# Experts' weight slots given back by their own last product, the spreading in two parts, and chunk-wise rows in the layers

## The chip, the core and the metric

The kernel runs on one core of one Trainium2 chip. The metric is the device time of one execution in microseconds (us), as the median of three runs. TensorE (PE) multiplies, VectorE (DVE) and ScalarE (ACT) move and transform what it leaves in the eight PSUM banks, GpSimd (POOL) does small steps of the norms, and SyncE (SP) issues the DMA transfers that bring the weights from HBM.

## The reference, cut to what matters

The input is x of 256 rows by 1024, and all numbers are fp32. First comes one block: a mixer, a cross attention to 256 rows of memory and a mixture of 32 experts, each added to x. Then come two layers, each with a mixer of three branches (a Hyena convolution, a gated linear attention, pooling) and a feed-forward part of width 2816, with norms before and after. The part on which most of this text turns is the mixture of experts, two of the 32 for each row:

```python
    expert_id = g_idx * EXPERTS_PER_GROUP + e_local
...
    def expert_block(args):
        xb, e = args
        return (jax.nn.silu(xb @ w_gate[e]) * (xb @ w_up[e])) @ w_down[e]
...
    contrib = (w_sorted[:, None] * y_disp[dest].astype(jnp.float32))
    out = jnp.zeros((T, D), jnp.float32).at[t_sorted].add(contrib)
```

An expert's w_gate and w_up are 1024x512 and its w_down is 512x1024, so that each expert has 6 MB of weights and all of them 192 MB.

## The kernel before

**The stages.** The first block up to its experts fills the first 272 us of the span, the experts follow until about 720 us, the first layer until 1203 us, the second until 1669 us, and a short end of norms and the store of the output closes it. Each engine has its program written out by hand. Between engines stand semaphores; the eight PSUM banks are handed out in turn by a recorder (`opened`, `close`, `taken_up`, `done`), whose waits the views of the order show as `filled` (TensorE is done with a bank) and `taken` (the bank has been read).

**The experts.** There are eight passes of four experts. Each expert takes at most 32 of its rows in a pass, so that the four of a pass lie side by side in four column groups of TensorE. The weights of a pass come in 12 slots of 2 MB: four for gate (c = 0 to 3), four for up, four for down (f = 0 to 3); each holds a quarter of that matrix for all four experts. The SP queue fills seven or more places in turn, and issues into a place once `w_used` of it is counted (L4403). On TensorE `expert_pass` does eight products a slot (`mm` with a 128x32 left side and 512 columns; kk = 0, 1 and the expert q = 0 to 3). A released slot is only put into a list (`release`), and the next product that passes through `first_mm` carries its signal.

**The fifth block of rows.** One expert of each pass, the fullest, gets a further block of 32 rows. VectorE copies this expert's part of each slot (128x1024, `more_slot`, L2814, semaphore `more_copied`), since which expert it is is known at run time only. `more_products` on TensorE (right side "const" or "zone") uses two such copies at a time and signals `more_used`, after which VectorE may copy the next two. TensorE waits for the copy of each slot before it gives the slot back:

```python
                    more_slot(4 * i + c)
                    release(at)
```

**Around the gate slots of passes 1 to 7** stand other steps: `in0` and `in1` gather the rows of the pass (VectorE scales `in1` in `rows_in`, L2876); `more_in` gathers those of the fifth block (32 products with 32 columns, evacuated on L2890); `spread` brings the results of the pass before back to their places in x, for row tile t = 0 and t = 1 (`own_rows`, `more_rows`), and `add_rows` on VectorE (L2972) adds them; `weights_T` transposes the weights of the rows, `weights_out` copies them (L2884) and then picks and weighs the rows of the next pass (`place`, L2736 and L2743); `more_weights` does so for the fifth block (L2782). Pass 7 has no such spreading in it, since pass 6 spreads its own at its end.

**The layers.** `quad` in `pe_layer` (L3168) is one step of a matrix product on halves: sums and row sums are made by VectorE (`sums`, `tsum`), partial products are held in SBUF by ScalarE (`held`, L3579). The norm ahead of the feed-forward part ("m") ends on VectorE with one scaling of 128x1024 for each row tile (L4183), TensorE transposes the tile into two banks (`norm_tile_T`), ScalarE copies these with the gain (four 128x128, L2003), and the products `ff20` and `ff21` of row tile 0 begin after both. The transposes of row tile 1 follow behind them. In the quad `QK_QUAD` ScalarE also does two Exp (L3608) and two Ln (L3611, `low_rank`) of 128x1024 between its held copies.

The functions that the diff touches:

## Time and profile before

| what | value |
|---|---|
| median of three runs (lowest, highest) | 1692.74 us (1691.36, 1692.76) |
| the profiled execution: its time, its span | 1691.05 us, 1688.9 us |
| TensorE busy | 1635.9 us, 97% of the span |
| VectorE busy, ScalarE busy | 60%, 19% |
| read from HBM | 395.22 MB |

The span is what the profile covers; the execution's time is 2.15 us longer. A busy TensorE is not one at its peak: the ends of its instructions are modelled, and products in different column groups overlap.

### The profile page before, as it was taken

How to read it: one execution, taken by the hardware profiler on the slowest of the kernel's cores; microseconds unless marked ns; L12 is line 12 of the kernel's file. 1: busy time of each engine (PE TensorE's matmuls, PEld its weight loads, DVE VectorE, ACT ScalarE, POOL GpSimd, SP SyncE). 2: the span in 40 equal slices, each digit the busy share in tenths (PEclk: the TensorE clock that was granted, in tenths of full speed). 3: DMA queues.
4: the chain of work that ended last, by engine and by line, in shares of the span. 5: the costliest groups of instructions: out<-in, count | busy, mean ns of one | idle time of the engine just before them, and what ended most of it. 6: DMA issues, size and time to landing. Idle time of an engine off the chain costs nothing. (4 is left out here: it accounts for less than half of the span.)

```text
span 1688.9 us, 26924 instructions
## 1 busy us (share of the span) xinstructions
PE 1635.9 (97%) x11364; PEld 1218.6 (72%) x11364; DVE 1010.8 (60%) x1654; ACT 324.9 (19%) x758; POOL 25.3 (1%) x49
## 2 busy tenths in 40 slices
PE   9999999999988999999999999999999999999998
PEld 8777975443433344398799969994798999699953
DVE  4767445344433433369656677766688566677675
ACT  2332222100000000113232122110233221121100
POOL 0010000000000000000000000000000000000000
PEclk9999999997998999999999999999999999999999
DMA  9323388999999999945322524533534143433540
GB/s 364 153 102 149 150 374 328 400 429 427 427 428 427 427 427 426 425 176 199 150 100 107 203 116 200 200 154 133 212 138 180 71 198 144 183 153 147 200 174 25
DMA packets 30635, 398.03 MB, mean 236 GB/s; under 512 B 3505, under 2 KB 4145, under 8 KB 5810
## 3 DMA queue, kind: packets, MB, share of 16 engines
q1 hardware_dynamic: 29938, 393.66, 57.1%
q10 hardware_dynamic: 576, 2.62, 0.4%
q8 instruction: 92, 1.51, 0.4%
q14 instruction: 29, 0.24, 0.0%
HBM read 395.22 MB, written 1.05 MB: 235 GB/s over the span
## 5 line engine op out<-in xcount | busy, mean ns | idle before, releaser
L1249 PE MATMUL bank<-zone,w 128*128 128x128 f32 (+1 forms) x5632 | 659.9, 279 | 4.7 <-ACT zone L2003 1.7
L1249 PEld LDWEIGHTS bank<-zone,w 128*128 128x128 f32 x5632 | 649.6, 192 | 15.2 <-issue 5.9
L1249 PE MATMUL bank<-zone 128*128 128x128 f32 (+7 forms) x3220 | 478.0, 415 | 11.4 <-DMA zone<-in_w_experts 4.0
L1249 PE MATMUL bank<-w,zone 128*32 128x512 f32 (+2 forms) x1736 | 425.1, 581 | 10.1 <-DMA w<-in_w_experts 8.3
L1249 PEld LDWEIGHTS bank<-zone 128*128 128x128 f32 (+2 forms) x3220 | 308.6, 169 | 169.0 <-issue 139.6
L1249 PEld LDWEIGHTS bank<-w,zone 128*128 128x128 f32 (+1 forms) x1736 | 197.6, 156 | 207.2 <-issue 183.7
L2012 ACT ACTIVATE zone<-bank 128x512 f32<-128x512 f32 (+2 forms) x97 | 52.7, 561 | 420.7 <-PE bank L1249 314.6
L3833 DVE TENSOR_TENSOR w<-w 128x1024 f32<-128x1024 f32 x88 | 103.5, 1218 | 0.0
L3579 ACT ACTIVATE zone<-bank 128x256 f32<-128x256 f32 x88 | 33.7, 385 | 216.9 <-PE bank L1249 216.9
L3841 DVE TENSOR_TENSOR zone<-bank,zone 128x256 f32<-128x256 f32 x88 | 36.3, 422 | 61.7 <-PE bank L1249 34.5
L2814 DVE TENSOR_SCALAR zone<-w 128x1024 f32 x52 | 34.8, 689 | 61.4 <-PE bank L1249 45.4
L3833 DVE TENSOR_TENSOR w<-zone,w 128x1024 f32<-128x1024 f32 x44 | 52.9, 1222 | 20.4 <-PE bank L1249 20.4
L1299 PEld LDWEIGHTS bank<-const,zone 128*128 128x128 f32 (+2 forms) x256 | 28.0, 146 | 41.1 <-DVE zone L2814 11.8
L3833 DVE TENSOR_TENSOR zone<-w 128x1024 f32<-128x1024 f32 x44 | 52.0, 1218 | 3.2 <-DMA w<-in_w_layers 3.1
L2814 DVE TENSOR_SCALAR zone<-zone 128x1024 f32 x42 | 28.2, 688 | 41.1 <-PE bank L1249 31.7
L1299 PE MATMUL bank<-const,zone 128*128 128x128 f32 (+2 forms) x256 | 37.5, 281 | 14.2 <-DVE zone L2814 5.7
L1249 PE MATMUL bank<-zone,const 128*32 128x512 f32 (+2 forms) x284 | 44.9, 643 | 4.3 <-DVE const L2890 4.3
L2972 DVE TENSOR_TENSOR x<-bank,x 128x512 f32<-128x512 f32 x32 | 20.6, 686 | 43.4 <-PE bank L1249 43.4
L3841 DVE TENSOR_TENSOR zone<-bank,held 128x256 f32<-128x256 f32 x44 | 18.5, 424 | 43.2 <-PE bank L1249 42.8
L3786 DVE TENSOR_SCALAR zone<-zone,vec 128x256 f32<-128x256 f32 x68 | 27.9, 410 | 14.1 <-ACT zone L3765 10.9
L4354 POOL TENSOR_TENSOR stat<-stat 128x1 f32<-128x1 f32 (+2 forms) x28 | 17.1, 612 | 1162.2 <-DVE stat L3025 456.4
L3788 DVE SCALAR_TENSOR_TENSOR zone<-zone,vec 128x256 f32<-128x256 f32 x68 | 33.0, 485 | 2.4
(321 smaller groups left out, 978.5 us busy)
## 6 DMA issues: line engine op xcount, KB each, us to landing
w<-in_w_layers SPq DMA_DIRECT2D x66, 2048.0 KB, 8.8
w<-in_w_experts SPq DMA_DIRECT2D x52, 2048.0 KB, 21.5
zone<-in_w_experts SPq DMA_DIRECT2D x42, 2048.0 KB, 23.4
w<-in_w_first SPq DMA_DIRECT2D x15, 2048.0 KB, 8.8
w<-in_w_layers SPq DMA_DIRECT2D x4, 1536.0 KB, 6.3
w<-in_w_layers SPq DMA_DIRECT2D x4, 1024.0 KB, 6.5
w<-in_w_first SPq DMA_DIRECT2D x2, 1024.0 KB, 7.1
zone<-in_w_split SPq DMA_DIRECT2D x2, 1024.0 KB, 8.7
```

The source lines that it names most:

```text
L1249: return eng.matmul(out, lhsT, rhs, start=start, stop=stop, **kw_)
L1299: ins = eng.transpose(bank[0:m, at:at + n], src, idn)
L2012: A(dst, src, func, **k).then_inc(*banks.done(pl, name))
L2814: V.tensor_scalar(more_part(pl.region, n), spots[at].rearrange("p (q n) -> p q n", q=EPI)[:, bass.ds(q, 1), :].rearrange("p a n -> p (a n) ...
L2972: V.tensor_tensor(xs, banks.tile(pl, f"{pre}{t}{n}"), xs, ALU.add).then_inc(*banks.done(pl, f"{pre}{t}{n}"))
L3579: A(carried[name][:, g], banks.tile(pl, f"sx{p}{g}")[:, 0:T].rearrange("p (i t) -> p i t", i=2), ACT.Copy).then_inc(*pl.up(sem("held")))
L3786: v(pl, V.tensor_scalar(dst, src[:, 0:T], pv(layer, wname, 3 * c), pv(layer, bname, c), ALU.mult, ALU.add))
L3788: V.scalar_tensor_tensor(dst, src[:, 2:T + 2], pv(layer, wname, 3 * c + 2), dst, ALU.mult, ALU.add).then_inc(*pl.up(signal))
L3833: V.tensor_tensor(to, l, r, op).then_inc(*pl.up(sem("sums")))
L3841: return V.tensor_tensor(quad_rows(p, g, second, t), bank, carried[name][:, g], ALU.add)
L4354: eng.tensor_tensor(rstd[:, at:at + n], ms[:, col:col + n], mhalf[:, 0:n], ALU.pow).then_inc(*pl.up(sem("rstd")))
```

## The change

**In the experts, on TensorE.** The wait for the copy of a slot stands before the slot's last product (q = 3 of kk = 1, in down q = 3 of the second half) and no longer behind it, and this last product itself signals `w_used`. The last slot of gate, of up and of down, whose last product closes a bank, still gives its slot back by the next product; with gate and up the wait moves there too, while with the last slot of down it stays behind.

**In the gate slots of passes 1 to 7.** Before, `spread` of both row tiles, `weights_T`, `more_in` and the first `more_products` stood between c = 1 and c = 2. Now only `more_in` stands there; the first `more_products` are within c = 2; `spread` of row tile 0 stands behind c = 2; the second `more_products`, `spread` of row tile 1 and `weights_T` stand behind c = 3. VectorE's steps follow this order. The results of the fifth block lie in another place until they are spread (`more_ye`).

**In the layers.** The quads wait for each row sum by itself. In norm "m" VectorE scales in halves, ScalarE signals each 128x128 of row tile 0 (`first_rows`), TensorE goes through `ff20` and `ff21` together, k by k, and the transposes of row tile 1 stand behind the first product group of the first up quad. The second Ln stands behind one held copy.

```diff
@@ -1774,31 +1776,41 @@
                         for evacuated in banks.taken_up(gp, f"in{c // 2}"):
                             eng.wait_ge(*evacuated)
                     for kk in range(2):
-                        if pass0 and (kind, c, kk) == ("gate", 3, 1):
+                        if (kind, c, kk) == ("gate", 3 if pass0 else 2, 1):
                             more_products(kind, part, 1)
                         for q in range(EPI):
                             r = q * CAP
+                            if (kk, q) == (1, EPI - 1):
+                                more_slot(4 * i + c)
                             ins = mm(bank[r:r + CAP, :], Xg[:, 2 * c + kk, r:r + CAP],
                                      w[:, q * 1024 + kk * FE:q * 1024 + (kk + 1) * FE], c == 0 and kk == 0, c == 3 and kk == 1)
-                            if (c, kk, q) < (3, 1, EPI - 1):
+                            if (kk, q) < (1, EPI - 1):
                                 first_mm(pl, ins)
                     if c == 3:
                         ins.then_inc(*banks.close(pl, kind))
-                    more_slot(4 * i + c)
-                    release(at)
+                    else:
+                        ins.then_inc(*pl.up(sem(f"w_used{at}")))
+                    if c == 3:
+                        release(at)
                     if pass0 and (kind, c) == ("up", 0):
                         weights_T(1)
-                    if not pass0 and (kind, c) == ("gate", 1):
+                    if not pass0 and kind == "gate" and c >= 2:
+                        if c == 3:
+                            more_products(kind, part, 3)
                         if spreading:
-                            spreading.pop()(pl, "prev")
-                        weights_T(0)
+                            spreading[0](pl, "prev", [c - 2])
+                        if c == 3:
+                            weights_T(0)
+                            if spreading:
+                                banks.skip(pl, 3)
+                            spreading.clear()
                     if (kind, c) == ("gate", 2 if pass0 else 1):
                         eng.wait_ge(*pl.need(sem("more_picked"), 1))
                         group(pl, "more_in", [((P, k * CAP, CAP), [(hs[:, t, k * P:(k + 1) * P], Pm_in[:, t, :]) for t in range(TT)])
                                               for k in range(KT)])
                     if c == (2 if pass0 and kind == "gate" else 1):
                         part = opened(pl, f"more_{kind}")
-                    if c % 2 == 1 and not (pass0 and (kind, c) == ("gate", 1)):
+                    if c % 2 == 1 and not (kind == "gate" and (c == 1 or not pass0)):
...
@@ -1807,14 +1819,18 @@
             bank = [opened(pl, f"down{n}") for n in range(2)]
             for evacuated in banks.taken_up(pl, "hid"):
                 eng.wait_ge(*evacuated)
-            def down_half(f, half, cols):
+            def down_half(f, half, cols, freeing=None):
                 for q in range(EPI):
                     r = q * CAP
+                    if f < 3 and (half, q) == (1, EPI - 1):
+                        more_slot(8 + f)
                     ins = mm(bank[half][r:r + CAP, :], hidT[:, f, r:r + CAP], cols(q), f == 0, f == 3)
-                    if f < 3 or q < EPI - 1:
+                    if q < EPI - 1 or (f, half) < (3, 0) and half == 0:
                         first_mm(pl, ins)
                 if f == 3:
                     ins.then_inc(*banks.close(pl, f"down{half}"))
+                elif half == 1:
+                    ins.then_inc(*pl.up(sem(f"w_used{freeing}")))
...
-            def spread(to, pre):
+            def spread(to, pre, tiles=range(TT)):
                 for evacuated in banks.taken_up(pl, "weights", "down0", "down1"):
                     eng.wait_ge(*evacuated)
-                for t in range(TT):
+                for t in tiles:
...
-                    down_half(f, half, lambda q: (kept, w)[half][:, q * 512:(q + 1) * 512] if split else w[:, q * 1024 + half * 512:q * 1024 + (half + 1) * 512])
-                more_slot(8 + f)
-                release(at)
+                    down_half(f, half, lambda q: (kept, w)[half][:, q * 512:(q + 1) * 512] if split else w[:, q * 1024 + half * 512:q * 1024 + (half + 1) * 512], at)
+                if f == 3:
+                    more_slot(8 + f)
+                    release(at)
...
@@ -2001,6 +2018,8 @@
                 if gname:
                     for c in range(4):
                         ins = A(dst[:, c, t * P:(t + 1) * P], bank[:, c, :], ACT.Copy, scale=pv(layer, gname, c))
+                        if (pre, t) == ("m", 0) and c < 3:
+                            ins.then_inc(*pl.up(sem("first_rows")))
...
@@ -2924,12 +2943,14 @@
                 rows_in(pl)
                 more_slot(pl, q, 0)
                 more_slot(pl, q, 1)
-                if i < PASSES - 1:
-                    add_rows(pl, banks, pre="prev")
+                more_in()
+                for t in range(TT):
+                    more_slot(pl, q, 2 + t)
+                    if i < PASSES - 1:
+                        add_rows(pl, banks, [t], "prev")
                 weights_out()
-                more_in()
                 more_weights(pl, e)
-                for n in range(2, 8):
+                for n in range(4, 8):
...
-                eng.wait_ge(*pl.need(sem("tsum"), 8 if p in UP_QUADS else 4))
+                eng.wait_ge(*pl.need(sem("tsum"), row_sum + 1))
...
@@ -3433,14 +3458,27 @@
         release(two[0])
         out_product(out_sums["S1"], tsum[:, 0], "l5")
         out_product(out_sums["S4"], rows[1, 1], "lo01")
-        norm_tile_T(pl, "m", hs, sem("hs"), 1, 0)
-        for evacuated in banks.taken_up(pl, "m0", "m1"):
-            eng.wait_ge(*evacuated)
+        norm_tile_T(pl, "m", hs, sem("hs"), 2, 0)
         ka, wa = slot(pl)
         kb, wb = slot(pl)
-        for j in range(2):
-            early(pl, f"ff{20 + j}", (wa, wb), (j * P, j * P), hT, 0, step=256)
-        norm_tile_T(pl, "m", hs, sem("hs"), 2, 1)
+        both = [opened(pl, f"ff{20 + j}") for j in range(2)]
+        for k in range(KT):
+            if k < 3:
+                eng.wait_ge(*pl.need(sem("first_rows"), k + 1))
+            elif k < 5:
+                for evacuated in banks.taken_up(pl, f"m{k - 3}"):
+                    eng.wait_ge(*evacuated)
+            for j, bank in enumerate(both):
+                for i, w in enumerate((wa, wb)):
+                    first_mm(pl, mm(bank[:, i * T:i * T + P], w[:, k * 256 + j * P:k * 256 + j * P + P], hT[:, k, 0:P],
+                                    (k, i) == (0, 0), k == KT - 1, skip_group_check=True))
+
+        def second_rows():
+            banks.skip(pl, NB - 3)
+            for half in range(2):
+                eng.wait_ge(*pl.need(sem("hs"), 3 + half))
+                transposes(pl, f"m{2 + half}", [(P, j * P, P, hs[:, 1, (4 * half + j) * P:(4 * half + j + 1) * P], ident) for j in range(4)])
+            banks.skip(pl, 1)
 
         def second_tile():
             for evacuated in banks.taken_up(pl, "m2", "m3"):
@@ -3450,8 +3488,10 @@
             release(ka)
             release(kb)
 
-        for p in UP_QUADS:
-            quad(p, second_tile if p == UP_QUADS[0] else None)
+        banks.skip(pl, 2)
+        quad(UP_QUADS[0], second_tile, second_rows)
+        for p in UP_QUADS[1:]:
+            quad(p)
...
@@ -3606,11 +3646,13 @@
             for r in range(2):
                 eng.wait_ge(*pl.need(sem("absf"), r + 1))
                 A(B[:, r, :], B[:, r, :], ACT.Exp).then_inc(*pl.up(astep))
-            for r in range(2):
-                eng.wait_ge(*pl.own(astep))
-                A(B[:, r, :], B[:, r, :], ACT.Ln, bias=1.0).then_inc(*pl.up(sem("lnf")))
-
-        carry(QK_QUAD, {("m1", 0): folded, ("m1", 1): low_rank})
+            forget(0)
+
+        def forget(r):
+            eng.wait_ge(*pl.own(astep))
+            A(B[:, r, :], B[:, r, :], ACT.Ln, bias=1.0).then_inc(*pl.up(sem("lnf")))
+
+        carry(QK_QUAD, {("m1", 0): folded, ("m1", 1): low_rank, ("u2", 0): lambda: forget(1)})
...
@@ -4180,6 +4222,11 @@
                             ).then_inc(*pl.up(sem("ms")))
             eng.wait_ge(*pl.need(sem("rstd"), pl.count(sem("ms"))))
             eng.wait_ge(*pl.own(signal))
+            if gain == 0:
+                for n in range(2):
+                    V.tensor_scalar(hs[:, t, 512 * n:512 * n + 512], x[:, t, 512 * n:512 * n + 512], rstd[:, t:t + 1], None, ALU.mult
+                                    ).then_inc(*pl.up(sem("hs")))
+                return
```

`carry` is the list of what ScalarE does behind each held copy of a quad.

TensorE in pass 2, from row tile 1 of the spreading to the next slot, before ("w,zone 32x512" are a slot's products; "zone,const 32x512" those of the fifth block; "128x512" the spreading; "128x32" is more_in; L1299 is a transpose, here weights_T):

```order
L1249 MATMUL bank<-zone 128x512 [waits taken5]
L1249 MATMUL bank<-zone 128x512 [waits taken6]
L1249 MATMUL bank<-zone 128x512 x2
L1299 MATMUL bank<-const,zone 128x128 [waits taken7,placed]
L1299 MATMUL bank<-const,zone 128x128
L1249 MATMUL bank<-zone 128x32 [waits more_picked]
L1249 MATMUL bank<-zone 128x32 x15
L1249 MATMUL bank<-zone,const 32x512 [waits taken0,taken1]
L1249 MATMUL bank<-zone,const 32x512 x3
L1249 MATMUL bank<-w,zone 32x512 [waits w_ready3]
L1249 MATMUL bank<-w,zone 32x512 x7
```

The same place in TensorE's order after the change, from the c = 3 slot to the first up slot:

```order
L1251 MATMUL bank<-w,zone 32x512 [waits w_ready4]
L1251 MATMUL bank<-w,zone 32x512 x6
L1251 MATMUL bank<-w,zone 32x512 [waits more_copied]
L1251 MATMUL bank<-zone,const 32x512 x4
L1251 MATMUL bank<-zone 128x512 [waits taken7]
L1251 MATMUL bank<-zone 128x512 x3
L1301 MATMUL bank<-const,zone 128x128 [waits placed]
L1301 MATMUL bank<-const,zone 128x128
L1251 MATMUL bank<-w,zone 32x512 [waits w_ready7,taken5]
L1251 MATMUL bank<-w,zone 32x512 x6
L1251 MATMUL bank<-w,zone 32x512 [waits more_copied]
```

`more_in` and the c = 2 slot no longer stand behind the spreading: row tile 1 follows the c = 3 slot, the transposes stand directly before the first up slot, and each slot has its wait for `more_copied` ahead of one last product.

VectorE in pass 2, from the last two adds to the next copy of a slot, before ("128x128" on L2736, L2743 and L2782 are place and more_weights, "128x1024" the copy of slot 2):

```order
L2972 TENSOR_TENSOR x<-bank,x 128x512 [waits filled6]
L2884 COPY zone<-bank 128x256 [waits filled7]
L2736 TENSOR_TENSOR zone<-zone 128x128 x2
L2743 TENSOR_TENSOR zone<-zone 128x128 [waits picked,vector_step]
L2743 TENSOR_TENSOR zone<-zone 128x128
L2890 TENSOR_TENSOR const<-bank,stat 128x256 [waits filled0]
L2782 ISA
L2782 TENSOR_SCALAR zone<-zone 128x128
L2782 ISA
L2782 TENSOR_SCALAR zone<-zone 128x128
L2814 REGISTER_ALU [waits w_ready7,more_used]
L2814 TENSOR_SCALAR zone<-w 128x1024
```

The same place of VectorE's order after the change (L2993, L2903, L2909 and L2833 are the lines that were L2972, L2884, L2890 and L2814; L2755, L2762 and L2801 those that were L2736, L2743 and L2782):

```order
L2993 TENSOR_TENSOR x<-bank,x 128x512 [waits filled7]
L2993 TENSOR_TENSOR x<-bank,x 128x512 [waits filled0]
L2903 COPY zone<-bank 128x256 [waits filled1]
L2755 TENSOR_TENSOR zone<-zone 128x128 x2
L2762 TENSOR_TENSOR zone<-zone 128x128 [waits picked,vector_step]
L2762 TENSOR_TENSOR zone<-zone 128x128
L2801 ISA
L2801 TENSOR_SCALAR zone<-zone 128x128
L2801 ISA
L2801 TENSOR_SCALAR zone<-zone 128x128
L2833 ISA [waits w_ready9,filled4]
L2833 TENSOR_SCALAR zone<-zone 128x1024
```

The evacuation of `more_in` (L2890) and the copies of slots 2 and 3 have come ahead of these rows, and what follows the adds, the copy of the weights and the 128x128 steps is now the copy of slot 4, the first of up.

TensorE at norm "m" of the first layer, from the second transposes of row tile 0 to the first up quad, before ("x15" and its like are ff20 and ff21):

```order
L1299 MATMUL bank<-const,zone 128x128 [waits taken4]
L1299 MATMUL bank<-const,zone 128x128 x3
L1249 MATMUL bank<-zone,w 128x128 [waits w_ready7,w_ready4,taken5,taken4,taken3]
L1249 MATMUL bank<-zone,w 128x128 x15
L1249 MATMUL bank<-zone,w 128x128 [waits taken6]
L1249 MATMUL bank<-zone,w 128x128 x15
L1299 MATMUL bank<-const,zone 128x128 [waits taken7,hs]
L1299 MATMUL bank<-const,zone 128x128 x3
L1299 MATMUL bank<-const,zone 128x128 [waits taken0]
L1299 MATMUL bank<-const,zone 128x128 x3
```

The same place after the change, from the wait for the third 128x128 of row tile 0 to behind the transposes of row tile 1:

```order
L1251 MATMUL bank<-zone,w 128x128 [waits first_rows]
L1251 MATMUL bank<-zone,w 128x128 x3
L1251 MATMUL bank<-zone,w 128x128 [waits taken3]
L1251 MATMUL bank<-zone,w 128x128 x3
L1251 MATMUL bank<-zone,w 128x128 [waits taken4]
L1251 MATMUL bank<-zone,w 128x128 x15
L1251 MATMUL bank<-zone,w 128x128 [waits taken1,w_ready8]
L1251 MATMUL bank<-zone,w 128x128 x7
L1301 MATMUL bank<-const,zone 128x128 [waits taken7,hs]
L1301 MATMUL bank<-const,zone 128x128 x3
L1301 MATMUL bank<-const,zone 128x128 [waits taken0,hs]
L1301 MATMUL bank<-const,zone 128x128 x3
```

The products follow ScalarE's copies one by one, and eight products of the quad stand between them and the transposes of row tile 1, whose two halves each wait for their own scaling.

## Rows read from the trace of the kernel before

**Rows 1.** The profile's page: busy time (share of the span) and instructions.

```profile
PE 1635.9 (97%) x11364; PEld 1218.6 (72%) x11364; DVE 1010.8 (60%) x1654; ACT 324.9 (19%) x758; POOL 25.3 (1%) x49
```

**Rows 2.** TensorE's waits, 272 to 720 us (us in total, times, longest).

```profile
PE bank L1249 <- DMA w<-in_w_experts: 8.3, 5, 3.1
PE bank L1299 <- DVE zone L2814: 5.7, 4, 2.1
PE bank L1299 <- DVE zone L2943: 4.8, 2, 2.5
PE bank L1249 <- DVE const L2890: 4.3, 7, 0.6
PE bank L1249 <- DMA zone<-in_w_experts: 4.0, 4, 1.4
```

**Rows 3.** Windows: busy us of five engines, granted clock, DMA share, GB/s.

```profile
378.00:436.00 58.00, 55.19 (x368) 23.77 (x367) 23.56 (x51) 4.73 (x11) 0.00 (x0) 0.82 1.01 428
```

**Rows 4.** TensorE's timeline near the end of pass 7 (start us, us).

```profile
697.37 3.64 PE L1249 MATMUL bank<-zone 128*32 128x512 f32 x32 [0.47 <-DMA zone<-in_w_experts]
702.27 3.64 PE L1249 MATMUL bank<-zone 128*32 128x512 f32 x32 [1.26 <-DMA zone<-in_w_experts]
```

**Rows 5.** VectorE's timeline in the gate slots of pass 2 (start us, us).

```profile
376.50 1.29 DVE L2972 TENSOR_TENSOR x<-bank,x 128x512 f32<-128x512 f32 x2 [1.68 <-PE bank L1249]
377.70 0.41 DVE L2884 COPY zone<-bank 128x256 f32<-128x256 f32 x1
378.03 0.48 DVE L2736 TENSOR_TENSOR zone<-zone 128x128 f32<-128x128 f32 x2
378.62 0.49 DVE L2743 TENSOR_TENSOR zone<-zone 128x128 f32<-128x128 f32 x2
...
380.97 0.59 DVE L2782 TENSOR_SCALAR zone<-zone 128x128 f32<-128x128 f32 x2
383.31 1.29 DVE L2814 TENSOR_SCALAR zone<-w 128x1024 f32 x2 [1.74 <-PE bank L1249]
```

**Rows 6.** TensorE's timeline over the same stretch and behind it.

```profile
376.40 0.44 PE L1299 MATMUL bank<-const,zone 128*128 128x128 f32 x2
376.67 3.92 PE L1249 MATMUL bank<-zone 128*128 128x32 f32 x32
381.20 1.94 PE L1249 MATMUL bank<-zone,const 128*32 128x512 f32 x8 [0.61 <-DVE const L2890]
382.88 5.55 PE L1249 MATMUL bank<-w,zone 128*32 128x512 f32 x32
...
389.14 3.64 PE L1249 MATMUL bank<-w,zone 128*32 128x512 f32 x32
```

**Rows 7.** VectorE's timeline at the first slot of pass 3.

```profile
424.36 1.13 DVE L2876 TENSOR_SCALAR zone<-bank,stat 128x128 f32<-128x128 f32 x4 [2.64 <-PE bank L1249]
425.40 0.68 DVE L2814 TENSOR_SCALAR zone<-w 128x1024 f32 x1
```

**Rows 8.** TensorE's timeline at the first slot of pass 3.

```profile
424.25 1.92 PE L1249 MATMUL bank<-w,zone 128*32 128x512 f32 x16
```

**Rows 9.** TensorE's waits in the layers, 720 to 1689 us.

```profile
PE bank L1249 <- ACT zone L2003: 2.0, 3, 0.8
PE bank L1249 <- ACT zone L3579: 1.4, 2, 0.7
PE bank L1299 <- DVE zone L4183: 1.3, 2, 0.7
```

**Rows 10.** Timeline of ScalarE at the two Ln.

```profile
778.70 2.01 ACT L3611 ACTIVATE zone<-zone 128x1024 f32<-128x1024 f32 x2
...
780.61 0.64 ACT L3579 ACTIVATE zone<-bank 128x256 f32<-128x256 f32 x2
```

**Rows 11.** Windows with a low granted clock (columns as in rows 3).

```profile
381.20:387.00 5.80, 5.80 (x32) 1.63 (x36) 1.66 (x4) 0.00 (x0) 0.00 (x0) 0.52 1.02 432
...
400.10:409.50 9.40, 9.37 (x40) 5.42 (x40) 3.99 (x9) 1.51 (x3) 0.00 (x0) 0.52 1.01 428
```

More of the change, by code:

```diff
@@ L399 @@
             'filled7': 17,
+            'first_rows': 3,
             'fpad': 2,
@@ L407 @@
             'hpad': 2,
-            'hs': 4,
+            'hs': 6,
             'kscaled': 2,
@@ L471 @@
             'filled7': 17,
+            'first_rows': 3,
             'fpad': 2,
@@ L479 @@
             'hpad': 2,
-            'hs': 2,
+            'hs': 4,
             'kscaled': 2,
@@ L608 @@
            'filled1': 3,
-           'filled2': 3,
+           'filled2': 2,
            'filled3': 2,
            'filled4': 2,
-           'filled5': 2,
+           'filled5': 3,
            'filled6': 2,
@@ L625 @@
            'taken1': 3,
-           'taken2': 3,
+           'taken2': 2,
            'taken3': 2,
            'taken4': 2,
-           'taken5': 2,
+           'taken5': 3,
            'taken6': 2,
@@ L648 @@
            'filled1': 3,
-           'filled2': 3,
+           'filled2': 2,
            'filled3': 2,
            'filled4': 2,
-           'filled5': 2,
+           'filled5': 3,
            'filled6': 2,
@@ L666 @@
            'taken1': 3,
-           'taken2': 3,
+           'taken2': 2,
            'taken3': 2,
            'taken4': 2,
-           'taken5': 2,
+           'taken5': 3,
            'taken6': 2,
@@ L687 @@
            'w_used9': 2},
- 'pass4': {'filled0': 3,
+ 'pass4': {'filled0': 4,
            'filled1': 3,
-           'filled2': 3,
-           'filled3': 3,
-           'filled4': 3,
+           'filled2': 2,
+           'filled3': 2,
+           'filled4': 2,
            'filled5': 3,
-           'filled6': 2,
-           'filled7': 2,
+           'filled6': 3,
+           'filled7': 3,
            'filter': 1,
@@ L703 @@
            'placed': 1,
-           'taken0': 3,
+           'taken0': 4,
            'taken1': 3,
-           'taken2': 3,
-           'taken3': 3,
-           'taken4': 3,
+           'taken2': 2,
+           'taken3': 2,
+           'taken4': 2,
            'taken5': 3,
-           'taken6': 2,
-           'taken7': 2,
+           'taken6': 3,
+           'taken7': 3,
            'vector_step': 9,
@@ L1213, in program @@
     more_x = cv("sel")[:, 0:KT * CAP].rearrange("p (k s) -> p k s", k=KT)
-    more_ye = sG
+    more_ye = hid
     dg = sG[:, 0:TT * P].rearrange("p (t s) -> p t s", t=TT)
@@ L3170, in quad @@
             S1 = late_sum if p >= GATE_QUADS[0] else early_sum
+            row_sum = 4 if p in UP_QUADS else 0
             rows = {(b, t): hT[:, 4 * b:4 * b + 4, t * P:(t + 1) * P] for b in range(2) for t in range(TT)}
@@ L3206, in quad @@
                 eng.wait_ge(*pl.need(sem("held"), step(HELD, "m1", g, p)))
+                eng.wait_ge(*pl.need(sem("tsum"), row_sum + 2))
                 product(g, A[g]["A11"], tsum[:, 1], banks.tile(pl, f"sx{p}{g}"), False)
@@ L3536, in pe_layer @@
             ahead[LAYER[layer + 1]] = pl
-            norm_tile_T(pl, "n", hs, sem("hs"), 3, 0)
+            norm_tile_T(pl, "n", hs, sem("hs"), 5, 0)
         summed_up(2, "S4")
```

2 lines of the change are left out of this document (added).

## The prediction

> **What bounds the kernel now.** I read the page first: TensorE is busy for 97% of the span [rows 1], so the question is where it still waits. The view of the waits splits these by what ends them. In the layers there are three kinds [rows 9]: ScalarE's copies ahead of `ff20` (L2003; 2.0 us, of which the two longest, of 0.8 each, are the ones that the change is at), the held copy behind the two Ln (L3579; two of 0.7), and the scaling of row tile 1 (L4183; two of 0.7). In the experts [rows 2] TensorE waits 8.3 + 4.0 = 12.3 us for slots, 4.3 us for the evacuation of `more_in` (seven times, one a pass from pass 1 on), and 5.7 us for copies of slots (L2814). The windows show the DMA engines full, at 428 GB/s [rows 3], and in pass 7 the last down slots are waited for [rows 4]. So two things are near each other: the train of transfers, and TensorE, which has only 12.3 us in 448 to spare. A slot's products take 3.64 us for two slots [rows 6], 1.73 us each from start to start; by that TensorE is fast, but spreading, gathering, `more_in` and the fifth block fill the rest of a pass.
>
> The profiled execution took 1691.05 us, 1.7 below the median. The sum is made against it, and 1.7 is added at the end.
>
> **The layers.** All four layer edits work at the waits of [rows 9]. The Ln behind a held copy: the two Ln take 2.01 us together and the held copy started as they ended [rows 10]; with one Ln ahead of it, it starts a full one earlier, and the wait of 0.7 goes. ScalarE's four 128x128 have a first product behind the first of them instead of the last: 0.8 goes. The transposes of row tile 1 have eight products of a quad ahead (16 of TensorE's records of a little over 0.1 us, about 1.8 us as an estimate) against a wait of 0.7, and half the scaling in addition: 0.7 goes. Twice (0.7 + 0.8 + 0.7) is 4.4 us. Bounds: 0 if the next input is late by as much, 4.4 as all there is. TensorE is busy without a break behind each of them, so I take 4.4. The row sums by chunk I cost at nothing: the sums S1 that the same products wait for stand behind all row sums on VectorE; that cover gone, it would still be only an earlier wait.
>
> **The experts, TensorE's new waits.** The question is when the copy is done by which the last product of a slot is now held. A slot is 1.73 us, its last product is half of that, 0.86, in its column group. If the copy ends H after the slot starts, the group ends at H + 0.86, and the stall is H − 0.86, once something of the whole array follows.
>
> *First gate slot.* The copy follows the four scalings of `in1`: it ends at 426.08 [rows 7], the slot starts at 424.25 [rows 8], H is 1.83 and the stall 1.0. Behind the slot the same wait cost about 0.15 before. Net +0.8.
>
> *Third gate slot.* The fifth block's products now lie inside it, and the copy waits for them. VectorE began 0.17 behind them (383.14 to 383.31 [rows 5, 6]) and takes 0.69: with the semaphore 0.9, all of it a stall. The wait for `more_in`'s evacuation, 0.6 [rows 2, 6], goes, since four products cover it. Net +0.3.
>
> *Fourth gate slot.* Its copy stands behind the adds of row tile 0, which begin when TensorE ends the spreading and starts the slot. Adds 1.29, copy 0.65: H is 1.95, the stall +1.1.
>
> *First up slot.* Its copy stands behind the adds of row tile 1, the copy of the weights, place and `more_weights`. From 376.50 the first four end at 378.62 + 0.49 = 379.11 [rows 5]; with 0.59 and 0.65 the copy would end at 380.3. TensorE has only the two transposes beside it (376.40 to 376.84 [rows 6]) and the slot. H is 380.3 − 376.84 = 3.5, the stall +2.65. Before, `more_in`'s 3.92 us of products [rows 6] lay beside this chain and hid it. This is the largest term, and the order shows it: what follows the last 128x128 steps is now the copy of slot 4.
>
> *Third up slot and second down slot.* A copy can begin only as the fifth block's products ahead end, the same 0.9 against 0.86: 0.3 and, with a step between, 0.5. Bounds 0 and 1.4, taken 0.8.
>
> The sum of a pass is 0.8 + 0.3 + 1.1 + 2.65 + 0.8 = 5.65 us. Six passes (1 to 6) give 33.9. Pass 7 has no adds: the fourth slot's term falls away and the up slot's falls by 1.29, which leaves 0.8 + 0.3 + 1.35 + 0.8 = 3.3, less the 0.5 of down, where slots are waited for anyway [rows 4]: 2.8. Pass 0 keeps its order: 2.0 for its first slots and down. Together 38.7 us.
>
> **Who waits for that.** Behind a held product stands everything on TensorE, and the slot's return to SP. The transfers have up to a ring of places ahead, so a later return costs nothing until TensorE's lag is a ring long. TensorE's delays are first taken out of its 12.3 us for slots. What is left is 38.7 − 12.3 = 26.4, less 4.4 in the layers: +22.0. 1691.05 + 22.0 + 1.7 is 1714.7; I say 1714 us.
>
> Here a rule bears on the price. The rows show four products side by side in 0.86 us [rows 6, 8]. The Trainium skill (TensorEngine Tiling (Array Packing), Key Properties) says that tiles operate independently of each other. By it a held product delays one column group, and the three others go on, as soon as it is issued; by that rule alone the stalls at the first gate slot and the fourth, where more products of this kind follow, would be shorter by 0.86 each for those three groups. The spreading and the gathering use the whole array, though, and collect the loss; the sum keeps it.
>
> **The rivals.** *Faster: the transfers stay the bound.* If a pass loses no more than (12.3 + 4.4 − 4.6) / 6 = 2.0 us on TensorE, nothing is lost: this is the point from which it decides. It would be so if the copy of the first up slot were not late, for instance since VectorE has run ahead of TensorE there. For it speaks that the DMA engines are full in every window; against it, that the adds can't start before the spreading ends [rows 5]. The time is 1692.7 − 4.4 = 1688.3; with the last slot's 1.3 [rows 4] landing earlier, since slots of the first passes are given back sooner, 1687.
>
> *Half lost.* The stalls are real but shorter, 3.5 us a pass (0.86 of three of them isn't collected): 21 + 4 − 12.3 − 4.4 = +8.3, 1701.
>
> *Slower still: the clock.* After the wait of 2.2 us for L2943 the granted clock was 0.52 for 9.4 us [rows 11], the lower of its levels, 1.2 GHz, and after `more_in` 0.52 for 5.8 us; two slots took 5.55 us there against 3.64 [rows 6]. If each of the six stalls of 2.65 us brings such a stretch over two slots, they cost 6 x 1.9 = 11.4 more: 1725. Against it: at other waits over 2 us it stayed high. The Trainium skill (TensorE: Matmul & The Clock Gate, What's actually happening) says that throttled is the default state and activity releases it; by that rule a longer stall makes the drop likelier, not certain, and the trace agrees with its two levels.
>
> *The layers give nothing*, since VectorE is late behind each wait: 1718, within the range.
>
> **How the numbers follow.** Forecast (1704 to 1720 with its own bounds) 0.48, clock 0.12, half lost 0.10 (1696 to 1704), between half lost and faster 0.06, faster 0.24 (its best part, below 1687, is 0.07). The range leaves out that part and most of the clock case, and with a tail of the forecast 0.2 in all: 1687 to 1724. About 0.2%, 3.4 us, is what a measurement here can tell from no change: faster 0.24, same 0.06, slower 0.70.
>
> **What would show it.** In the waits of the experts: L2814 (now L2833) ahead of TensorE's slot products, some 2 to 3 us once a pass in passes 1 to 6, at the first up slot, and about 1 us at the fourth gate slot; the wait for `more_in` gone; the waits for slots nearly gone, and the DMA share under 1 in the later passes. In the layers the three waits of [rows 9] down to a few tenths. The stage's end would move from about 720 to some 745 us. It is wrong if the waits for slots remain as they are, which would say that TensorE's work was never near the bound; or if VectorE's chain behind the adds is hidden by something that I have missed.

## The result, and the profile after

The changed kernel takes 1703.49 us (median of 4; 1702.19 to 1706.30) beside 1692.12 us for the kernel before: a ratio of 1.0061, 95% interval 1.0046 to 1.0075, 11.4 us slower by the medians, 10.3 by the ratio. The forecast was slower by 21.9 us, to 1714; the sign was right and the size about twice too large.

The page of the profiled execution (1702.78 us), against [rows 1]:

```profile
span 1700.6 us, 26922 instructions
...
PE 1659.0 (98%) x11364; PEld 1224.8 (72%) x11364; DVE 1009.2 (59%) x1658; ACT 324.5 (19%) x758; POOL 25.3 (1%) x49
```

TensorE's waits in the experts after, against [rows 2] (us in total, times, longest):

```profile
PE bank L1251 <- DVE zone L2833: 15.7, 10, 2.1
PE bank L1301 <- DVE zone L2964: 4.2, 2, 2.3
PE bank L1251 <- ACT zone L2031: 3.8, 6, 0.9
```

L2833 is the copy of a slot, L2814 before. Its waits have grown from 5.7 to 15.7 us: the 10.0 us more are six waits of 1.6 to 2.0, one a pass at the first up slot of passes 1 to 6. At the fourth gate slot, for which the forecast had a wait of about 1 us, the trace has only 0.13 us of idle time; what that slot costs shows in experiments 3 and 4. The waits for slots (8.3 and 4.0 us) and for `more_in` (4.3 us) are gone, and so are 2.2 us that the view before puts to "issue", once, at 662 us:

```profile
PE bank L1249 <- issue: 2.2, 1, 2.2
```

TensorE is the bound of the whole stage now. In the layers, against [rows 9]:

```profile
PE bank L1251 <- DVE zone L4326: 0.4, 2, 0.2
PE bank L1251 <- issue: 0.4, 1, 0.4
```

All three kinds of waits there are gone. At the first up slot of pass 2, TensorE and then VectorE, against [rows 5, 6]:

```profile
398.66 0.44 PE L1301 MATMUL bank<-const,zone 128*128 128x128 f32 x2
399.03 1.92 PE L1251 MATMUL bank<-w,zone 128*32 128x512 f32 x14
402.54 2.33 PE L1251 MATMUL bank<-w,zone 128*32 128x512 f32 x17 [1.60 <-DVE zone L2833]
404.29 0.60 PE L1251 MATMUL bank<-zone,const 128*32 128x512 f32 x3
404.71 0.59 PE L1251 MATMUL bank<-w,zone 128*32 128x512 f32 x1
```

```profile
398.76 1.29 DVE L2993 TENSOR_TENSOR x<-bank,x 128x512 f32<-128x512 f32 x2 [4.96 <-PE bank L1251]
399.96 0.41 DVE L2903 COPY zone<-bank 128x256 f32<-128x256 f32 x1
400.29 0.48 DVE L2755 TENSOR_TENSOR zone<-zone 128x128 f32<-128x128 f32 x2
400.88 0.49 DVE L2762 TENSOR_TENSOR zone<-zone 128x128 f32<-128x128 f32 x2
401.29 0.59 DVE L2801 TENSOR_SCALAR zone<-zone 128x128 f32<-128x128 f32 x2
401.80 1.29 DVE L2833 TENSOR_SCALAR zone<-w 128x1024 f32 x2
```

The slot starts at 399.03 with 14 of its 16 records (two records a product), and the last product starts at 402.54, 3.5 us later, when the copy has ended: the H of 3.5 that the forecast had. While it is held nothing behind it on TensorE starts. Then the other groups go on to the next slot's products while its own has this one still to do, and it stays behind by one product, 0.86 us: at 404.29 three groups begin with the fifth block's products, and at 404.71 the fourth is still at the slot's. No wait in the list shows that. The stage itself, the windows of before and after (columns as in [rows 3]):

```profile
272.00:721.00 449.00, 415.41 (x2954) 180.12 (x2954) 171.16 (x371) 41.96 (x94) 1.07 (x2) 0.93 1.00 422
```

```profile
272.00:738.00 466.00, 439.58 (x2963) 186.78 (x2963) 170.11 (x372) 42.71 (x96) 1.07 (x2) 0.97 0.98 409
```

The stage is 17 us longer, where the forecast's own sum had 26.4. And something moved that it had held fixed: the granted clock of the stage rose from 0.93 to 0.97. With two levels, 0.07 below full is 63 us of 449 at the lower one, 0.03 is 28 of 466.

### The profile page after: what moved, and what is told of

The parts are those of the page before. It is cut to its first block, busy times and chain, and to the rows that moved or that the text cites. A ratio compares the mean times of both kernels' runs of the same rounds, so it can differ in the third digit from the quotient of the medians.

```text
span 1700.6 us, 26922 instructions
## 1 busy us (share of the span) xinstructions
PE 1659.0 (98%) x11364; PEld 1224.8 (72%) x11364; DVE 1009.2 (59%) x1658; ACT 324.5 (19%) x758; POOL 25.3 (1%) x49
## 4 chain that ended last, share of the span: by engine, by line
PE 90%; DVE 6%; issue 2%; ACT 1%; POOL 0%; DMA 0%; DVEq 0%; POOLq 0%
PE bank L1251 88%; PE bank L1301 2%; DVE zone L2833 1%; DVE x L2993 1%; DVE zone L4304 0%; DVE zone L4326 0%; DVE zone L3829 0%; DVE zone L3830 0%; POOL stat L4401 0%; DVE zone L2507 0%; ACT zone L2031 0%; DMA x<-in_x 0%; DVE zone L2755 0%; DVE zone L3828 0%; DVE w L2335 0%
## 5 line engine op out<-in xcount | busy, mean ns | idle before, releaser
L1251 PE MATMUL bank<-zone 128*128 128x128 f32 (+7 forms) x3220 | 506.4, 415 | 10.9 <-DVE zone L2833 4.2
L1251 PE MATMUL bank<-w,zone 128*32 128x512 f32 (+2 forms) x1736 | 451.5, 560 | 14.0 <-DVE zone L2833 11.5
L1251 PEld LDWEIGHTS bank<-zone 128*128 128x128 f32 (+2 forms) x3220 | 316.0, 168 | 176.9 <-issue 135.6
L1251 PEld LDWEIGHTS bank<-w,zone 128*128 128x128 f32 (+1 forms) x1736 | 201.9, 153 | 216.9 <-issue 163.9
L1251 PE MATMUL bank<-zone,const 128*32 128x512 f32 (+2 forms) x284 | 61.0, 612 | 0.0
L2993 DVE TENSOR_TENSOR x<-bank,x 128x512 f32<-128x512 f32 x32 | 20.6, 686 | 61.6 <-PE bank L1251 61.6
L2833 DVE TENSOR_SCALAR zone<-w 128x1024 f32 x52 | 34.7, 687 | 35.0 <-PE bank L1251 34.9
L2833 DVE TENSOR_SCALAR zone<-zone 128x1024 f32 x42 | 28.2, 687 | 30.1 <-PE bank L1251 30.1
## 6 DMA issues: line engine op xcount, KB each, us to landing
w<-in_w_experts SPq DMA_DIRECT2D x52, 2048.0 KB, 14.8
```

What stands on the lines that cost most here:

```text
L1251: return eng.matmul(out, lhsT, rhs, start=start, stop=stop, **kw_)
L2833: V.tensor_scalar(more_part(pl.region, n), spots[at].rearrange("p (q n) -> p q n", q=EPI)[:, bass.ds(q, 1), :].rearrange("p a n -> p (a n) ...
L2993: V.tensor_tensor(xs, banks.tile(pl, f"{pre}{t}{n}"), xs, ALU.add).then_inc(*banks.done(pl, f"{pre}{t}{n}"))
```

## The experiments

Each is compared with the kernel before in the same job (medians of 1692.7 to 1694.5 us). Two theories stood at first. By the first, the loss comes from the order of the gate slots, which leaves VectorE's chain (the adds, the copy of the weights, place and `more_weights`) open ahead of the first up slot; by the second, from the held product alone, which leaves its column group behind in any order.

**1. The layers alone** (`e1_layers`; all edits of `pe_layer`, the norm and the Ln, none of the experts').

```diff
-        norm_tile_T(pl, "m", hs, sem("hs"), 1, 0)
+        norm_tile_T(pl, "m", hs, sem("hs"), 2, 0)
...
+        quad(UP_QUADS[0], second_tile, second_rows)
```

> The layer edits alone (row sums by chunk, halves and k by k at norm m, the moved transposes, the second Ln behind a held copy), the experts as before. If the three waits of TensorE in the layers were all there is and nothing is late behind them, 4.4 us less than before: 1687.7, with the three kinds of waits gone. If VectorE or ScalarE is late by as much behind them, no change: 1692.

1689.18 us, 0.9971 (0.9960 to 0.9982): 4.9 us less. TensorE's waits in the layers of this run are those that the changed kernel has:

```profile
PE bank L1251 <- issue: 0.4, 1, 0.4
PE bank L1251 <- DVE zone L4309: 0.4, 2, 0.2
```

**2. The experts alone** (`e2_experts`; the other hunks).

```diff
-    more_ye = sG
+    more_ye = hid
...
+                            if (kk, q) == (1, EPI - 1):
+                                more_slot(4 * i + c)
```

> The experts' part of the change alone, the layers as before. If the two parts are independent, this is the whole change's 1703.5 plus the 4.4 us of the layers: 1708. If the layers' gain isn't there, 1703.5.

1708.61 us, 1.0089 (1.0074 to 1.0105): 15.1 us more. With the layers' 4.9 less this is 10.2, against 11.4 for the whole: the parts add up.

**3. Only the wait and the return** (`e3_wait_only`), in the order of before.

```diff
+                            if (kk, q) == (1, EPI - 1):
+                                more_slot(4 * i + c)
...
+                    else:
+                        ins.then_inc(*pl.up(sem(f"w_used{at}")))
-                    more_slot(4 * i + c)
-                    release(at)
```

> Only the wait for the copy before a slot's last product, which itself gives the slot back; order of the gate slots as before. Theory 1 (the loss is the order, in which VectorE's chain lies open ahead of the first up slot): the held products cost 0.8 at the first gate slot, 0.3 at the third up slot, 0.5 to 1.3 in down, about 2 us a pass, 15 in all on TensorE; of these 12 are taken out of its waits for slots, 1692 to 1696. Theory 2 (the loss is that a held product leaves its column group 0.86 late, whatever the order): most of the loss of 16 us is here, 1702 to 1708. The granted clock shows whether this part lowers the low time of 64.7 us of before (mean 0.979) to that of the whole change (0.990).

1698.56 us, 1.0026 (1.0017 to 1.0035): 4.4 us more, between what the two theories gave.

**4. Only the order** (`e4_order_only`), wait and return as before.

```diff
-                    if not pass0 and (kind, c) == ("gate", 1):
+                    if not pass0 and kind == "gate" and c >= 2:
...
+                            spreading[0](pl, "prev", [c - 2])
```

> Only the new order of the gate slots on TensorE and VectorE; the wait for a copy stays behind its slot and the slot is given back by the next product. Theory 1: TensorE stops about 1.8 us behind the first up slot in passes 1 to 6, gains 0.6 at more_in: 8 us on TensorE in all, mostly taken out of its waits for slots, and the sum with the other part passes them; 1690 to 1696 alone, so that neither part alone costs much but both do. Theory 2: no loss, 1690. If instead the order itself costs (a later spreading), 1700 and more.

1693.13 us, 1.0000 (0.9990 to 1.0011). Neither part costs more than 4.4 us, both together 15.1. Windows over the gate and up slots of pass 6 show why; columns as before, in this order the kernel before, only the wait, only the order, the changed kernel:

```profile
602.80:633.80 31.00, 30.39 (x210) 11.64 (x207) 11.62 (x25) 0.60 (x1) 0.00 (x0) 0.89 1.01 428
```

```profile
610.70:643.00 32.30, 31.69 (x210) 12.60 (x210) 11.64 (x25) 0.60 (x1) 0.00 (x0) 0.89 1.01 428
```

```profile
608.50:638.60 30.10, 28.31 (x211) 10.19 (x209) 11.55 (x25) 0.60 (x1) 0.00 (x0) 1.00 1.01 429
```

```profile
618.70:652.50 33.80, 32.00 (x211) 10.87 (x211) 11.55 (x25) 0.60 (x1) 0.00 (x0) 1.00 0.98 409
```

The wait alone adds 1.3 us at the same clock (0.89). Order and wait together take 3.7 more than order alone, both at full clock, though TensorE is idle for 1.8 us in each (33.80 − 32.00 and 30.10 − 28.31): the 3.7 are in the busy time, as groups that lag. The timelines of the last two windows (only the order first, then the changed kernel) show the second spreading and the transposes of hid behind the last up slot:

```profile
624.68 3.04 PE L1249 MATMUL bank<-zone 128*128 128x512 f32 x8
...
638.57 0.66 PE L1299 MATMUL bank<-const,zone 128*128 128x128 f32 x4
```

```profile
637.56 3.04 PE L1251 MATMUL bank<-zone 128*128 128x512 f32 x8
...
652.47 0.66 PE L1301 MATMUL bank<-const,zone 128*128 128x128 f32 x4
```

From the window's start the changed kernel needs 18.9 us to the spreading where order alone needs 16.2, and 33.8 to the transposes where order alone needs 30.1. By the starts of single instructions the difference grows in four steps, each time that work of the whole array follows slots: 0.8 us at `more_in`, 1.0 at the first spreading, 0.8 at the second, 1.0 at the transposes of hid. In the order of before, slots are followed by such work only twice in this stretch (the spreading behind c = 1 and the transposes of hid), and the wait alone costs 0.9 and 0.4 us there. So both theories hold a part: the lag is collected, once for each step of the whole array behind slots, and the new order has four of these for two.

**5 and 6. The transfers halved** (`e5_half_before`, `e6_half_after`), in the kernel before and in the changed one. Only half of each expert slot is brought in passes 1 to 7; the other columns hold older weights.

```diff
+                cols = rows.shape[1] // (2 if pl.region in PASS[1:] else 1)
-                eng.dma_start(spots[at][:, 0:rows.shape[1]], rows)
+                eng.dma_start(spots[at][:, 0:cols], rows[:, 0:cols])
```

> The kernel before with only the left half of each expert slot transferred in passes 1 to 7 (the other columns hold older weights, so the output is another). The transfers are then far from the bound, and the time shows TensorE's own work. Theory A (what the forecast missed is the low clock: it falls from 64.7 to about 30 us of low time by the change's own order, and is worth half of its time once TensorE is the bound): without the 12.3 us of waits for slots this kernel still has 50 us or more of low clock and takes 1680, and the changed kernel treated alike takes 1702, 22 more. Theory B (the low clock of before comes from the waits for slots): they go, the low time falls to 30 us here too, and this kernel takes about 1665, 37 less than the changed one.

> The changed kernel with the same half transfers in passes 1 to 7. If TensorE is its bound throughout, as the trace has no wait for a slot, nothing changes: 1703, clock 0.990. If the transfers still hold it somewhere, 2 us and more less. Its distance to the kernel before with half transfers is what the change costs TensorE, with the clock: 22 by theory A, 37 by theory B.

1673.72 us (0.9886, 0.9861 to 0.9910) and 1704.77 us (1.0066, 1.0049 to 1.0083). The changed kernel doesn't notice that half of its transfers are gone. The kernel before is 19.2 us faster without the other half, where its waits for slots were 12.3. The interval of its ratio puts that between 15 and 24 us, above the 12.3 in any case. So the change costs TensorE 31.0 us, and 19.2 of these the transfers had covered: 11.8, the 11.4 measured. The low clock doesn't come from the waits for slots: they are gone in the fifth run, and the clock of its stage is as low as before:

```profile
272.00:703.00 431.00, 410.97 (x2957) 178.82 (x2956) 170.50 (x371) 42.15 (x95) 1.07 (x2) 0.93 0.65 239
```

The changed kernel with half the transfers:

```profile
272.00:742.00 470.00, 443.48 (x2959) 188.48 (x2959) 169.69 (x370) 42.42 (x96) 1.07 (x2) 0.96 0.62 219
```

Theory A was right that the low time stays at about 60 us; its distance of 22 us was too small, B's of 37 too large: between the two, 31.0 was measured.

**7. The chain behind the copies** (`e7_chain_behind`), in the changed kernel.

```diff
+                for n in range(4, 6):
+                    more_slot(pl, q, n)
                 weights_out()
                 more_weights(pl, e)
-                for n in range(4, 8):
+                for n in range(6, 8):
```

> The changed kernel, but VectorE copies slots 4 and 5 ahead of the copy of the row weights, place and more_weights. If that chain is what holds the last product of the first up slot, H falls from 3.5 to 1.95, and each of passes 1 to 6 is 1.5 us shorter: 9 us less, 1694, with the wait of 1.6 us at the first up slot gone. Theory 2 (the column group's lag, not the chain): the lag of 0.86 stays, and 1.5 or more of the stall remains, 1699 or above.

1695.81 us, 1.0018 (1.0008 to 1.0028): by the ratios 7.3 us less than the changed kernel, where 9 were expected. The wait at the first up slot is gone, the waits for copies fell from 15.7 to:

```profile
PE bank L1251 <- DVE zone L2833: 6.3, 4, 2.1
```

and the gate and up slots of pass 6 from 33.80 us to 31.90, at the same full clock:

```profile
616.30:648.20 31.90, 31.70 (x210) 11.14 (x210) 11.55 (x25) 0.60 (x1) 0.00 (x0) 1.00 1.00 422
```

1.9 us a pass, more than the 1.5 expected; what is missing in the total fits the low clock, which is back in other passes (0.986 as the median of ten executions, 0.990 in the changed kernel; in the profiled executions 17 us more at the lower level).

**8. Layers, order and early copies, with wait and return as before** (`e8_order_layers_chain`): the changed kernel less the third experiment's edit, plus the seventh's.

```diff
-                            if (kk, q) == (1, EPI - 1):
-                                more_slot(4 * i + c)
...
+                    more_slot(4 * i + c)
+                    release(at)
...
+                for n in range(4, 6):
+                    more_slot(pl, q, n)
```

> The layer edits and the new order of the gate slots, with the copies of slots 4 and 5 ahead of VectorE's chain, and each slot's wait and return as in the kernel before (behind the slot, with the next product). By the runs so far, order alone costs nothing and the layers bring 4.9: 1688 to 1689; if the order's stall at the first up slot had eaten a gain of the earlier issue of slots, up to 2 less: 1686.

1686.77 us, 0.9963 (0.9949 to 0.9977), with its repetition (the twelfth run) the lowest time of a kernel that brings all weights. Its gate and up slots of pass 6:

```profile
602.20:631.10 28.90, 28.30 (x211) 10.27 (x207) 11.63 (x25) 0.60 (x1) 0.00 (x0) 1.00 1.01 428
```

The seventh run's window has the same copies and the same clock of 1.00, and 31.70 us busy where this one has 28.30: 3.4 us for the moved wait with early copies, beside the 3.7 with late ones. The same kernel's second run (the twelfth) has 30.00 us at 0.94 for this stretch, about 28.2 at full clock by the reckoning further below, and so 3.7 less than the seventh:

```profile
606.40:636.40 30.00, 29.80 (x212) 10.93 (x211) 11.55 (x25) 0.60 (x1) 0.00 (x0) 0.94 1.01 428
```

So the moved wait costs as much whether the copies of slots 4 and 5 are early or late, and the chain costs 1.9 us a pass beside it. The eighth run's waits for slots, 14.8 us, are more than before the change: TensorE is faster here, and the transfers keep the end.

```profile
PE bank L1251 <- DMA w<-in_w_experts: 11.3, 7, 3.1
...
PE bank L1251 <- DMA zone<-in_w_experts: 3.5, 3, 1.8
```

**9. Work in TensorE's idle time** (`e9_half_warm`), on the kernel of the fifth run.

```diff
+                if pl.region in ("pass1", "pass2"):
+                    keep_warm(bank, 8, ident)
+                for evacuated in banks.taken_up(pl, "up"):
+                    eng.wait_ge(*evacuated)
...
+                        if pl.region in ("pass4", "pass5"):
+                            keep_warm(bank, 8, ident)
+                        more_slot(8)
```

> The kernel before with half transfers (as in the fifth run, 1673.7), and eight products of 128x128 without a use put into four of TensorE's waits of 2 us and more: ahead of the transposes of hid in passes 1 and 2, and ahead of more_weights in passes 4 and 5. They change no wait, since TensorE stands still there. If the idle time is what lowers the clock behind it and the low clock costs half of its time, the stretches behind these waits (3.4, 13.6 and 6.8 us in that run's records) go, and the time falls by up to 12 us, to 1662 or above. If the low stretches have another cause, 1674 with the same clock of 0.981.

1670.26 us beside 1673.72 (on another chip), with ranges (1666.72 to 1671.72, 1668.10 to 1677.64) that overlap: inconclusive in the total, and 12 us were not there. Behind the filled waits the traces are clear. The down slots of passes 2 and 4 in the fifth run, then in this one:

```profile
399.30:423.50 24.20, 24.20 (x156) 11.90 (x160) 7.43 (x17) 4.11 (x10) 0.00 (x0) 0.72 0.68 251
503.20:529.40 26.20, 24.11 (x166) 11.89 (x166) 10.43 (x18) 3.70 (x9) 0.00 (x0) 0.87 0.72 265
```

```profile
402.70:423.50 20.80, 19.48 (x156) 9.88 (x160) 7.42 (x17) 4.12 (x10) 0.00 (x0) 0.92 0.80 293
503.30:526.20 22.90, 22.79 (x178) 12.39 (x182) 10.43 (x18) 3.70 (x9) 0.00 (x0) 1.00 0.81 303
```

3.4 and 3.3 us less, with the clock from 0.72 to 0.92 and from 0.87 to 1.00. In the gate slots of other passes the clock fell instead, so that the mean went only from 0.981 to 0.982.

**10 to 12. What the order adds to the layers** (`e10_order_layers` is the eighth without its early copies; `e11_layers_again` the first, `e12_order_layers_chain_again` the eighth once more; beside each other on one chip).

```diff
-                for n in range(4, 6):
-                    more_slot(pl, q, n)
                 weights_out()
                 more_weights(pl, e)
-                for n in range(6, 8):
+                for n in range(4, 8):
```

> The eighth run without the moved copies: layer edits and new order, waits and returns as before, VectorE's chain ahead of the copy of slot 4 as in the change. If the chain costs TensorE 2 us a pass that the transfers mostly hide, 1688 to 1689; if the eighth run's 6.1 us less come from the layers alone, 1687 too.

> The layer edits alone once more, beside the next on the same chip: 4.9 us less than before, as in the first run.

> The eighth run's kernel once more: 6.1 us less than before, as there. If the order with the moved copies adds nothing to the layers, the two runs lie within 1 us of each other; if the slots given back earlier bring what they can, this one is 1 to 2 us below.

1687.58 (0.9966, 0.9952 to 0.9979), 1688.00 (0.9973, 0.9962 to 0.9984) and 1686.70 us (0.9965, 0.9951 to 0.9978). All intervals overlap. The layers bring 4.7 us; what order and early copies bring beyond them, 1.3 here and 1.4 by the ratios of the first and the eighth run, is not told from nothing. Nor is what the late chain costs where the transfers are the bound, 0.9 us between the tenth and the twelfth run.

## Why the prediction was right in sign and wrong in size

**Right.** The layers: 4.4 forecast, 4.9 and 4.7 measured. The largest stall: at the first up slot, H of 3.5 from the chain of VectorE, was found in place and size, and the seventh run shows that chain to be its cause. That the wait for `more_in` goes, that the waits for slots are used up, and that TensorE becomes the bound were seen as forecast. The stage's DMA share of 0.98 for 1.00 is the trace of it.

**The step that failed** is "Who waits for that": "TensorE's delays are first taken out of its 12.3 us for slots". The cover was 19.2 us (kernel before less fifth run), not 12.3, and these 6.9 us are the larger part of the 10.5 by which the forecast missed. A list of waits for slots holds only the time in which TensorE stands idle for a reason that the trace names. The profiled executions of the two kernels differ by 18.1 us (spans of 1688.9 and 1670.8). Of these, 12.3 are the listed waits; 2.2 are the wait put to "issue", which the fifth run doesn't have either (what it waits for, the trace doesn't tell); and the fifth run has 58.0 us at the lower clock where the kernel before has 64.9, which at half the time is 3.4. That makes 17.9.

**The term of the stalls** was 38.7 us and came out about right by luck. With no transfers in the way the change costs the experts 31.0 + 4.9 = 36 us, but this is the difference of two sizes that the sum had wrong. To compare stretches at different clocks I take their length times the clock as the length at full clock, an estimate that holds where TensorE is busy. The changed kernel shows it on the gate and up slots of passes 3 and 4, with the same work and the same 1.8 us idle, 1.7 us apart, where 35.40 at 0.95 would give 33.6:

```profile
433.50:468.90 35.40, 33.59 (x211) 11.39 (x207) 12.79 (x33) 0.60 (x1) 0.00 (x0) 0.95 1.01 428
489.60:523.30 33.70, 31.91 (x210) 10.83 (x210) 11.54 (x25) 0.60 (x1) 0.00 (x0) 1.00 1.01 427
```

In passes 1 to 6 the kernel before was never at 1.00 over these slots. Its 31.00 us at 0.89 would be 27.6, and pass 3 of the fifth run agrees with 29.50 at 0.94, or 27.7:

```profile
423.50:453.00 29.50, 28.89 (x211) 10.89 (x211) 12.90 (x33) 0.60 (x1) 0.00 (x0) 0.94 0.53 189
```

So these slots cost 6.1 to 6.2 us more a pass where the forecast's terms for them (0.8, 0.3, 1.1, 2.65 and 0.3) make 5.15. The steps are 0.6 for the new order with early copies (28.2), 1.9 for the chain (30.1) and 3.7 for the moved wait (33.8). Chain and moved wait, 5.6 together, were forecast well: the 5.15 are 5.75 without the 0.6 taken off for `more_in`. The order's own cost had no term: it takes up that 0.6 and 0.6 more. Over the stage, the windows of the fifth and the sixth run (431.00 at 0.93 and 470.00 at 0.96) are 401 and 451 at full clock: 50 us, an estimate, where the forecast had 38.7. What lies outside the gate and up slots of passes 1 to 6, some 13 of these where the forecast had 7.8, was not taken apart.

Against that stood a gain that no term had: the clock. The median clocks of the fifth and the sixth run, 0.9805 and 0.989, are 28 us less at the lower level, worth 14; 50 less 14 is the 36. With all transfers it is alike: the stage of the kernel before spent some 63 us at the lower level, that of the changed one 28. The forecast carried these stretches over unchanged, and its rival "slower still: the clock" had them grow, from the row behind the wait of 2.2 us [rows 11]. They shrank.

The sum by the runs is then: TensorE's cost in the experts 36, less 4.9 in the layers, less 19.2 that the transfers had hidden: 11.9. The case "half lost" gave 1701, nearer the result, but for the reason of lags that aren't collected; experiments 3, 4, 7 and 8 show that they are collected. The 4.6 us in the rival "faster" should be 4.8 (2.8 for pass 7 and 2.0 for pass 0), which leaves its 2.0 us a pass as it is.

**The rule on tiles.** The Trainium skill (TensorEngine Tiling (Array Packing), Key Properties) says that tiles operate independently. The trace agrees once the held product has started: at 404.29 three groups are a product ahead of the fourth. While it is held the others get nothing new, since it stands ahead of their next products in TensorE's order (1.60 us idle), and the lag comes back at the next step that uses the whole array, 0.8 to 1.0 us each time.

**What stays open** is why the low clock shrank. It isn't the waits for slots (fifth run). As medians of their executions the kernel before has 0.978, order alone and the wait alone 0.983 each, and both together (second run) 0.990. The executions of one kernel scatter too (kernel before 0.975 to 0.985 over 23 of them, with 1696.35 and 1689.87 us at the ends), and the eighth and the twelfth run, one kernel, have 54.6 and 64.9 us at the lower level in their profiles, so that a part of the profile's low stretches is chance. For the changed kernel 0.988 took 1706.30 us and 0.991 took 1702.19. The ninth run shows that filling a wait removes the low stretch behind it, and not that it removes low time on the whole.

## What to carry to other kernels

When a delay is to be absorbed by another engine's or the DMA's slack, don't take the slack from the list of waits: halve the transfers in a run, and the difference is the cover. Before a wait is moved ahead of the work that covered it, write down for each place when its releaser ends by the new order; a copy with a chain ahead of it must be moved with the wait. A held product among column groups costs more than its idle time shows, once for each step of the whole array that comes behind slots, so count these steps in the new order, and compare lengths of stretches at the same granted clock, not waits.

## What the runs showed of the hardware that was not expected

The granted clock differs with the order of the work, without any change in what is computed: 0.978 before, 0.983 with the new order or the moved wait alone, 0.990 with both. Where TensorE is the bound it shows in the time: the same gate and up slots of the changed kernel took 35.40 us at 0.95 and 33.70 at 1.00, and the down slots of pass 2 took 24.2 us at 0.72 and 20.8 at 0.92, with the same 156 records of TensorE. A longer idle time didn't mean a lower clock: the changed kernel is idle for 1.6 to 2.0 us once in each of six passes where the kernel before was for 0.6, and its clock is higher.
